# The expert products of the second block, split in three: one ring of raw weights, first loads during routing, a scatter by pair

## The reference, cut to what matters

```python
def hierarchical_moe(h, w_rg, b_rg, w_re, b_re, w1, w3, w2):
    g_prob = softmax(xt @ w_rg + b_rg);  g_idx = argmax(g_prob)
    e_logits = (xt @ w_re + b_re) of that group
    top_p, top_i = lax.top_k(softmax(e_logits), 2)
    comb = g_w * top_p / sum(top_p)
    # pairs of token and expert sorted by expert: 2 * 512 = 1024 pairs, 32 experts
    y = (silu(x_blk @ w1[e]) * (x_blk @ w3[e])) @ w2[e]      # 1024 -> 512 -> 1024
    out[token] += comb * y
```

## Time and profile before

| | |
|---|---|
| Time before, median of 3 runs | 3486.35 us (3483.95 to 3493.56) |
| The profiled execution | 3482.88 us, of which its span is 3481.1 |
| TensorE busy | 2897.5 us (83%) |
| DVE / ACT / POOL busy | 1648.9 / 951.3 / 851.2 us |
| HBM read / written | 609.23 / 48.30 MB |
| Products of the experts, up (line 2344) | 1024 records, 452.1 us busy |
| Products of the experts, down (line 2365) | 512 records, 225.1 us busy |

### The profile page before, as it was taken

The page is one execution under the profiler, slowest core; times in us unless marked ns, Lnnn a source line. Parts: engine busy times, 40 slices in busy tenths (PEclk is TensorE's granted clock), DMA queues, the critical chain, the costliest instruction groups (busy, mean ns, idle before and its releaser), DMA issues. The chain is left out here.

```text
span 3481.1 us, 33394 instructions
## 1 busy us (share of the span) xinstructions
PE 2897.5 (83%) x12218; PEld 2132.6 (61%) x12218; DVE 1648.9 (47%) x2849; ACT 951.3 (27%) x1583; POOL 851.2 (24%) x661
## 2 busy tenths in 40 slices
PE   4976876657499999999999986984797699999995
PEld 2444665446389999988888875753676344444442
DVE  4334558999556666666666665326321100000002
ACT  2014431135333333332333224243332010111111
POOL 0000113366434443433332322411211100000001
PEclk7988988878699999999999998997897799999998
DMA  7610012205577777777667652210210699999995
GB/s 225 228 41 16 25 50 85 73 0 143 168 276 278 271 281 282 274 264 253 244 249 258 247 187 75 95 51 4 73 49 27 251 335 334 334 335 335 335 329 192
DMA packets 293587, 658.83 MB, mean 189 GB/s; under 512 B 32236, under 2 KB 99564, under 8 KB 292972
## 3 DMA queue, kind: packets, MB, share of 16 engines
q1 hardware_dynamic: 245884, 485.59, 39.1%
q0 software_dynamic: 42992, 155.23, 13.3%
q10 hardware_dynamic: 4608, 16.78, 1.2%
HBM read 609.23 MB, written 48.30 MB: 189 GB/s over the span
## 5 line engine op out<-in xcount | busy, mean ns | idle before, releaser
L2344 PE MATMUL bank<-w,moe_xt 128*128 128x512 f32 x1024 | 452.1, 595 | 2.4 <-DMA w<-in_w 2.4
L1457 PE MATMUL bank<-h_hi,u_hi 128*128 128x384 f32 x1024 | 350.8, 343 | 50.7 <-DVE u_lo L1529 50.6
L1457 PE MATMUL bank<-h_hi,u_lo 128*128 128x384 f32 x1024 | 347.5, 339 | 0.0
L1457 PE MATMUL bank<-h_lo,u_hi 128*128 128x384 f32 x1024 | 346.8, 339 | 0.0
L1529 DVE TENSOR_TENSOR u_lo<-u_in,u_hi 128x1024 fp32r<-128x1024 f32 x128 | 156.6, 1223 | 382.3 <-ACT u_hi L1497 382.3
L2395 DVE TENSOR_TENSOR moe_xt<-bank,moe_gain 128x512 f32<-128x512 f32 x64 | 41.3, 687 | 623.8 <-PE bank L2334 623.8
L2344 PEld LDWEIGHTS bank<-w,moe_xt 128*128 128x128 f32 x1024 | 192.8, 191 | 233.4 <-issue 230.4
L209 POOL TENSOR_TENSOR w_lo<-ring,w_hi 128x512 fp32r<-128x512 f32 (+1 forms) x136 | 173.1, 1307 | 561.4 <-ACT w_hi L199 561.4
L1469 PE MATMUL bank<-v_hi,peer_w_lo 128*128 128x512 f32 x768 | 300.0, 391 | 0.0
L1469 PE MATMUL bank<-v_lo,peer_w_hi 128*128 128x512 f32 x768 | 299.9, 390 | 0.0
L1469 PE MATMUL bank<-v_hi,peer_w_hi 128*128 128x512 f32 x768 | 298.7, 389 | 0.0
(11 more groups left out here) (466 smaller groups left out, 5038.0 us busy)
## 6 DMA issues: line engine op xcount, KB each, us to landing
w<-in_w SPq DMA_DIRECT2D x64, 2048.0 KB, 19.4
u_in<-in_u_tiles SPq DMA_DIRECT2D x128, 512.0 KB, 8.7
v_in<-in_expert_v SPq DMA_DIRECT2D x128, 512.0 KB, 8.0
w_slot<-in_w SPq DMA_DIRECT2D x32, 2048.0 KB, 10.0
ada_in<-in_w_ada SPq DMA_DIRECT2D x48, 512.0 KB, 4.9
gates_by_key<-spread SPq DMA_DIRECT2D x3, 8192.0 KB, 30.6
gate_in<-gates_by_key SPq DMA_DIRECT2D x128, 192.0 KB, 8.1
ring<-in_w_in SPq DMA_DIRECT2D x11, 2048.0 KB, 8.1
```

What stands on the lines that cost most here:

```text
L1457: last = pe.matmul(g.bank[e][:, 0:DENSE_T], u[:, e, c], h[:, k, :], start=(n == 0), stop=(n == 3 * DC - 1))
L2344: last = pe.matmul(g.bank[2 if which == 1 else 3][:, :], self.xt[:, par, k, :], self.w13[par][0 if which == 1 else 1][:, k, :], start=(k = ...
```

## The change

The mixture is written anew around the same mathematics:

- **Products in three.** w1, w3 and w2 of each expert, the rows and z are split in hi and lo. ACT makes all hi tiles; DVE makes the lo tiles of w1, w3, the rows and z; POOL makes those of w2 (`down_low`). Weights are split in four pieces of 128x1024 each. TensorE does 72 fp32r products an expert for 24 float32 ones.
- **One ring of three raw buffers**, 2 MB each (`raw`), in the order w1 n, w3 n, w2 n-1. A buffer is loaded again as soon as its lo tiles are made. Hi and lo tiles are there once for each kind.
- **Whole rows.** Partition p takes rows 8p to 8p+7 (w2: 4p to 4p+3), one piece of 16 KB; the transposes take every eighth (fourth) column to fit.
- **First loads during routing.** The first three loads are issued by SyncE in `route` (`begin`).
- **Empty slots skipped.** The table is cleared with a number beyond all rows, and gather and scatter have a bound, so a slot without a pair moves nothing. POOL clears the row buffers once.
- **Scatter by pair.** The table holds the number of the pair (choice times 512 plus token). x is stored twice so that it can be gathered by pair, y is scattered to the pair's row by POOL (in place of ACT's plain store), and `finish` reads y with eight plain loads from SyncE. The DVE steps that made `result` go.
- y is copied out of PSUM by DVE, not ACT. All 32 experts are written out, without loops.

```diff
-                sp.dma_start(x_rows.rearrange("(i p) d -> p i d", p=P), xn_tiles[:, :, :]).then_inc(s["q_x"], 16)
+                for c in range(2):
+                    sp.dma_start(x_rows[c * T:(c + 1) * T, :].rearrange("(i p) d -> p i d", p=P), xn_tiles[:, :, :]).then_inc(s["q_x"], 16)
+                sp.dma_start(gain[:, :], g.a["norm_ffn_g_2"][0].rearrange("(p k) -> p k", k=DC)).then_inc(s["q_gain"], 16)
...
+                begin(sp)
...
-                pool.memset(zero[:, :], 0.0).then_inc(s["q_zero"], 1)
+                pool.memset(zero[:, :], ABSENT).then_inc(s["q_zero"], 1)
...
-                step(dve.tensor_copy(at_row[:], place[:]))
...
-                step(dve.tensor_scalar(blk[:], at_row[:], float(P), None, ALU.is_ge))
-                for b in range(2, CAP // P):
-                    step(dve.scalar_tensor_tensor(blk[:], at_row[:], float(b * P), blk[:], ALU.is_ge, ALU.add))
-                step(dve.scalar_tensor_tensor(at_row[:], blk[:], float((NE - 1) * P), at_row[:], ALU.mult, ALU.add))
-                step(dve.scalar_tensor_tensor(at_row[:], e_num[:], float(P), at_row[:], ALU.mult, ALU.add))
-                step(dve.tensor_copy(result[:, :, :], at_row[:].rearrange("p i c -> p c i")))
...
+def load_expert(sp, a, raw, raw_in, u):
+
+    n, kind = EXPERT_LOADS[u]
+    src = a[("w1_2", "w3_2", "w2_2")[kind]][0, n]
+    k = FC if kind == 2 else DC
+    sp.dma_start(raw[u % RAW][:, :, :].rearrange("p k n -> p (k n)").rearrange("p (k n) -> p k n", k=k),
+                 src.rearrange("(p k) n -> p k n", k=k)).then_inc(raw_in[u % RAW], 16)
...
+        hi, lo = ([sb(f"ex_w_{n}{i}", [P, CH, D], F32R) for i in range(3)] for n in ("hi", "lo"))
+        rows = g.ht[:, 0:4, :].rearrange("p (b k) t -> p b (k t)", b=2)
+        y = g.ht[:, 4:8, :].rearrange("p (b k) t -> p b (k t)", b=2)
+        xt = sb("row_t", [P, DC, P])
+        xt_hi, xt_lo = sb("row_t_hi", [P, DC, P], F32R), sb("row_t_lo", [P, DC, P], F32R)
+        z = sb("ex_z", [P, FE])
...
+                for u in range(RAW, len(EXPERT_LOADS)):
+                    n, kind = EXPERT_LOADS[u - RAW]
+                    if kind == 2:
+                        sp.wait_ge(s["r_lo2"], (n + 1) * CH)
+                    else:
+                        sp.wait_ge(s["r_lo"], up_chunks(n, kind, CH - 1))
+                    load_expert(sp, a, raw, raw_in, u)
...
+                def gather(n):
+                    if n >= 2:
+                        pool.wait_ge(s["r_xt"], 2 * (n - 1))
+                    pool.indirect_dma_start(out=rows[:, n % 2, :], out_offset=None, in_=x_rows,
+                                            in_offset=bass.IndirectOffsetOnAxis(ap=slots[:, n * BLOCKS:n * BLOCKS + 1], axis=0),
+                                            bounds_check=2 * T - 1, oob_is_err=False).then_inc(s[f"r_x{n % 2}"], 16)
+
+                def scatter(n):
+                    pool.wait_ge(s["r_yc"], 2 * n + 2)
+                    pool.indirect_dma_start(out=y_rows, out_offset=bass.IndirectOffsetOnAxis(ap=slots[:, n * BLOCKS:n * BLOCKS + 1], axis=0),
+                                            in_=y[:, n % 2, :], in_offset=None,
+                                            bounds_check=2 * T - 1, oob_is_err=False).then_inc(s[f"r_st{n % 2}"], 16)
+
+                def down_low(n):
+                    u = EXPERT_LOADS.index((n, 2))
+                    for c in range(CH):
+                        pool.wait_ge(s["r_hi"], 2 * CH + n * 3 * CH + 2 * CH + c + 1 if n < NE - 1 else 3 * CH * NE - CH + c + 1)
+                        pool.tensor_tensor(lo[2][:, c, :], whole(u, c), hi[2][:, c, :].bitcast(F32), ALU.subtract).then_inc(s["r_lo2"], 1)
+                pool.memset(g.ht[:, 0:4, :], 0.0).then_inc(s["r_zero"], 1)
+                pool.wait_ge(s["r_zero"], 1)
+                for n in range(2):
+                    gather(n)
+                for n in range(NE):
+                    if n + 2 < NE:
+                        gather(n + 2)
+                    down_low(n)
+                    scatter(n)
                 for par in range(2):
...
+                def up(n, which):
+                    if which == 0:
+                        pe.wait_ge(s["r_xlo"], n + 1)
+                    if n:
+                        pe.wait_ge(s["r_act" if which == 0 else "r_z"], n)
+                    for k in range(DC):
+                        if k % 2 == 0:
+                            pe.wait_ge(s["r_lo"], up_chunks(n, which, k // 2))
+                        at = slice(k % 2 * BANK, (k % 2 + 1) * BANK)
+                        for m, (x, w) in enumerate(((xt_hi, hi), (xt_lo, hi), (xt_hi, lo))):
+                            last = pe.matmul(g.bank[2 + which][:, :], x[:, k, :], w[which][:, k // 2, at], start=(k == 0 and m == 0), stop=(k == DC - 1 and m == 2))
...
+                flip_rows(0)
+                for n in range(NE):
+                    up(n, 0)
+                    if n:
+                        flip_z(n - 1)
+                    if n + 1 < NE:
+                        flip_rows(n + 1)
+                    up(n, 1)
+                    if n:
+                        down(n - 1)
...
+                weights_hi(0, 0)
+                rows_hi(0)
+                weights_hi(0, 1)
+                for n in range(NE):
+                    act.wait_ge(s["r_h1"], n + 1)
+                    if n:
+                        act.wait_ge(s["r_zt"], n)
+                    act.activation(z[:, :], g.bank[2][:, :], ACT.Silu).then_inc(s["r_act"], 1)
+                    if n:
+                        z_hi(n - 1)
+                    if n + 1 < NE:
+                        weights_hi(n + 1, 0)
+                        rows_hi(n + 1)
+                        weights_hi(n + 1, 1)
+                    weights_hi(n, 2)
...
+                weights_lo(0, 0)
+                rows_out(0)
+                rows_lo(0)
+                weights_lo(0, 1)
+                for n in range(NE):
+                    if n:
+                        z_lo(n - 1)
+                    if n + 1 < NE:
+                        rows_out(n + 1)
+                        weights_lo(n + 1, 0)
+                    dve.wait_ge(s["r_act"], n + 1)
+                    dve.wait_ge(s["r_h3"], n + 1)
+                    dve.tensor_tensor(z[:, :], g.bank[3][:, :], z[:, :], ALU.mult).then_inc(s["r_z"], 1)
+                    if n + 1 < NE:
+                        rows_lo(n + 1)
+                        weights_lo(n + 1, 1)
+                    if n:
+                        y_out(n - 1)
...
+                for i in range(TT):
+                    for c in range(2):
+                        row = c * T + i * P
+                        sp.dma_start(got[:, c, i, :], y_rows[row:row + P, :]).then_inc(s[f"t_g{i}"], 16)
```

More of the change, by code:

```diff
@@ L2125, with route @@
 RG = NG + NE
-def route(g, xn_tiles, x_rows, table, slot, result, weight, slots, over):
+ABSENT = float(1 << 20)
+RAW = 3
+def route(g, begin, gain, xn_tiles, x_rows, table, slot, weight, slots, over):
     nc, a = g.nc, g.a
@@ L2160, in route @@
         whole8 = [P, TT, 8]
-        with stage(nc, "q_w q_pool q_ready q_zero q_mm q_dve q_pair q_red q_exp q_exp2 q_hits q_pos q_slot q_sent q_clear q_rows q_flip q_x") as (block, s):
+        with stage(nc, "q_w q_pool q_ready q_zero q_mm q_dve q_pair q_red q_exp q_exp2 q_hits q_pos q_slot q_sent q_clear q_rows q_flip q_x q_gain") as (block, s):
             @block.sync
@@ L2333, in flip_rows @@
             for k in range(4):
[L2334 removed]
+                last = pe.transpose(g.bank[b][:, k * P:(k + 1) * P], self.rows[:, par, bass.ds(4 * b + k, P, step=DC)], g.ident[:, :])
             last.then_inc(s["r_xt"], 1)
@@ new lines, in store, with expert_loads @@
+        pool.wait_ge(s["r_yc"], 2 * n + 2)
+        pool.sem_inc(s["r_paced"], 1)
+        pool.indirect_dma_start(out=self.y_rows, out_offset=bass.IndirectOffsetOnAxis(ap=self.idx[:, par:par + 1], axis=0),
+                                in_=self.y[:, par, :], in_offset=None,
+                                bounds_check=2 * T - 1, oob_is_err=False).then_inc(s[f"r_st{par}"], 16)
+def expert_loads():
+    order = [(0, 0), (0, 1)]
+    for n in range(1, NE):
+        order += [(n, 0), (n, 1), (n - 1, 2)]
+    return order + [(NE - 1, 2)]
@@ L2555, in _ @@
         def _(pool):
+            pool.memset(m.rows[:, :, :], 0.0).then_inc(s["r_zero"], 1)
+            pool.wait_ge(s["r_zero"], 1)
             guarded(pool, gather)
@@ L2568, in _, with finish @@
             guarded(dve, gates)
-def finish(g, result, weight, y_rows, over, out):
+def finish(g, weight, y_rows, out):
     nc, a = g.nc, g.a
@@ L2590, in _ @@
                 sp.wait_ge(s["t_stored"], 16 * TT)
-            @block.gpsimd
-            def _(pool):
-                def gather(rows):
-                    for n in range(2 * TT):
-                        if n >= 4:
-                            pool.wait_ge(s["t_add"], n - 3)
-                        i, c = n // 2, n % 2
```

(25 more changed lines are left out.)

223 lines of the change are left out of this document (128 added, 95 removed).

## The result

The changed kernel takes **3615.93 us** (median of 4 runs, 3613.88 to 3616.54), the kernel before 3489.95 on the same chip (3483.95 to 3496.4): ratio 1.036, 95% interval 1.0338 to 1.0381. The forecast was 3544 and slower. The sign is right, the size is not: +126 us where +58 was forecast, 4 us above the range. The profiled execution took 3613.88, its span is 3612.1. Before, the span was 3481.1, so the traces are 131.0 apart.

A forecast was written before the change was run, and what follows sets the result against it. A ring through POOL's order and DVE was to bound the changed kernel at 24.0 us an expert: stage 12 + 31 x 24.0 + 23.4 = 779.4 (+60), routing and tail -2, 3541, with 3.5 for the median 3544; range 3442 to 3612.

The forecast's parts named there:

- TensorE's and ACT's work: Expert stage, per expert after the change: TensorE 18.2 us of products and transposes, ACT at most 16.8 us of copies.
- the loads: Expert stage: 6.55 MB an expert at 383 GB/s take 17.1 us, under TensorE's 18.2.
- rival 2: Expert stage: TensorE sets the pace, 18.2 to 19.5, with near-free scatter and gather and DVE unblocked; 3364 to 3405, chance 0.10.
- POOL's price: Expert stage: one POOL subtraction of 128x1024 for w2 takes 2.34 us, ends 2.28 and 3.19; four make 9.4.
- rival 3: Expert stage, slower still: scatter and gather issued during DVE's subtractions, period 26, or 27 with POOL at 3.19; 3606 to 3637, 0.15.
- The lock: Expert stage: DVE and POOL block each other when DVE reads two SBUF operands; the pair needs 19.6 us an expert.
- some DVE subtractions over 2 us: Expert stage: sign that the forecast is right; no DVE subtraction stretched would point to Rival 1.
- The rows land some 4.0 us after the issue ends: Expert stage, gathered rows: 3.5 us from a tail gather, 5.0 from the earlier median as the other end.
- the landing hardly matters between 3 and 5 us: Expert stage: POOL's subtractions keep DVE out anyway, so DVE, ready 8.6 us after the scatter's start, gets in at 9.5.
- Hand-overs: Expert stage, last part of one turn, with gate, low half of rows, w3 subtractions and y: 0.3 us.
- Ends of the stage and tail: Stage start 12 us, 0 against before; last expert's first product to last copy 23.4; routing and tail together -2 us.
- Rival 1: Expert stage: the ring without the lock, 21.7 us a turn, 20.7 with a landing of 3.0; 3442 to 3473, chance 0.15.

The follow-up runs named there:

- e6: e5 with the two copies of y an expert moved from DVE to the end of ACT's round: 3371.2 us, ratio 0.967 to the kernel before.
- e1: Changed kernel with POOL issuing the gather of expert n+3 ahead of scatter n, three gathers ahead of the loop: 3530.9 us.
- e2: Changed kernel with POOL's four w2 subtractions on 128 columns instead of 1024, the low half of w2 left out: 3629.7 us.
- e7: Changed kernel with each load from the fourth on bringing half its bytes (1 MB instead of 2): 3567.5 us.
- e9: Changed kernel with the load after DVE's last w3 subtraction issued only when TensorE has turned the next rows, all bytes loaded: 3566.2 us.
- e4: Changed kernel with 20 more unread fp32r products on TensorE between the transposes of z and the wait for rows: 3597.4 us.
- e5: Changed kernel with the gather order of e1 and the four w2 subtractions moved from POOL to the end of DVE's round: 3379.6 us.
- e10: Changed kernel with only the four w2 subtractions moved from POOL to the end of DVE's round, gather still behind the scatter: 3657.2 us.

## Why the prediction was right in sign and short in size

- **What bounded the kernel before, TensorE's and ACT's work, the loads**: as said. Fp32r products stand 0.23 apart at full clock, ACT's copies take 1.05 (bound 1.2), ACT waited for a load once, 4.3 us. The best version, e6, reaches rival 2's pace without rival 2's conditions: its 17.8 is close to the 18.2 that the prediction gave TensorE alone.
- **POOL's price**: 2.34 forecast, 2.37 measured. Scatter and gather: 2.5 against 2.35 (3019.01 to 3021.36). The issues fell into DVE's wait, not beside its subtractions, so rival 3 came out with its time (3606 to 3637) but not by its mechanism.
- **The lock**: right, and shown by e1, e2 and e7. In the kernel after, DVE's first four take from 4.6 us, the unhindered time, up to 6.9. The sign that the prediction named, "some DVE subtractions over 2 us", came: the longest took 3.46, though their group's mean is only 1.30. The sign doesn't tell what the lock costs.
- **The step that failed: the landing, followed along DVE alone.** "The rows land some 4.0 us after the issue ends", from a gather in the tail without loads about it, with the earlier trace rows at 5.0 as the other end. It is 6.3 in the median (7.3 - 1.0), beyond both ends. And "the landing hardly matters between 3 and 5 us" holds at the values measured (e7, e9: 3.0 to 3.3 after the issue's end, turn 24.48), but I stopped there: I had followed the rows to DVE alone. Followed along TensorE, through the transposes to the w3 product and the gate, with the half clock that TensorE has behind its wait, the landing limb passes the other at an estimated 5.6 us from the gather's start (16.1 - 1.3 - 1.6 - 7.6). Turns with 6.4 and 6.5 still got by, as fewer of their products ran slowly. At full clock it would pass at an estimated 8.1 (16.1 - 1.3 - 6.2, and 0.5 from the last product's start to the gate), and the measured 7.3 would have cost almost nothing. In 29 turns the gate waited 32.4 us for TensorE, 1.1 a turn, and the low half of the rows 9.4 us for ACT, which stands behind the same product.
- **Hand-overs**: 0.3 forecast for those behind the gate, but y's end to scatter alone is 0.81. The part behind the gate is 8.4 with nobody waiting (e7: 3021.96 to 3030.32), forecast 7.9, and 8.8 in the mean of the kernel after, partly for that wait for ACT. DVE's limb ends at 16.3 in the mean, 0.2 late. So 24.0 + 1.1 + 0.9 + 0.2 = 26.2.
- **TensorE's clock** is no term of the prediction. It had TensorE wait nearly 6 us a round and priced its products at the 0.23 of full clock all the same. Some eight products a turn take 0.43, inside the limb. In the 18 turns of e4 that keep the clock, the whole 1.7 us between 26.2 and 24.5 are gone; over all 29 it is 0.8.
- **Ends of the stage and tail**: start 2.95 late where 0 was forecast: the slots were there at 2725.2, but clearing, issue and landing, transposes and splits lasted to 2738.92, 15.4 instead of 12 after 2723.56. Behind the last copy +0.4 instead of -2: the plain loads did save time (8 sums in 11.0 us), but from the last scatter's issue to the first instruction of the next stage 9.3 us pass (3574.33 to 3583.66).
- **Rival 1** (the ring without the lock) named the right ring, with a landing of 3 to 4 us; at the true 6.3 it gives 24.0 as well, without lock or TensorE's limb. That the forecast's range missed by only 4 us says little for it: it had no case in which both landing and lock counted.

## What to carry over

When two chains leave the same event and meet again, price both, by every engine that stands between, with the clock that its waits leave it, and give the landing of a gather the traffic that the change itself puts beside it. A gather that is used in the turn in which it is issued belongs ahead of every instruction that waits, and this comes before balancing the engines: here the balance alone lost 41 us, behind the right order it won 151.

## What the chip showed that I had not expected

- A gather lands 3.0 us after its issue's end with one load held back (e9), 6.3 with it ahead, 7.9 where a second load leaves 2.8 us behind the gather (e2). Pieces of 2 and 4 KB or of 16 KB: 6.0 and 6.3.
- DVE and POOL don't share the loss. POOL's subtraction keeps 2.37 to 2.43 us, DVE's goes from 1.22 to 2.66 (10.65 over four).
- The other way round POOL can lose: in e5 the scatter is issued while DVE does its four subtractions for w2, and takes 4.62 us instead of 1.00:

```profile
3011.34 4.62 DVE L2620 TENSOR_TENSOR ex_w_lo<-expert_raw,ex_w_hi 128x1024 fp32r<-128x1024 f32 x4
...
3012.23 4.62 POOL L2481 DMA_INDIRECT moe_y_rows<-ht,slots  x1 [12.40 <-DVE ht L2627]
```

  The Trainium skill, page "SBUF — State Buffer", section "SBUF: two separate sides", tells of such a starved issue for DVE's faster modes; here it happens beside operations with two float32 operands out of SBUF. They don't always cost that much: beside the same four in e10 the scatter took 1.21 (at 3031.61) and the gather 1.99, and no run shows why e5's takes 4.62.
- Strided columns in a transpose cost nothing: eight in 1.05 at full clock (at 2745.97), 1.04 in the earlier trace rows.
